# Two long attentions: row maxima taken in parts of 512 keys from two shared banks, keys loaded earlier, and a chunk's end moved to later steps of VectorE

## The reference, cut to what matters

```python
def gqa_attend(q, k, v):
    s = jnp.einsum('bqhgd,bkhd->bhgqk', q, k).astype(jnp.float32) * (GQA_HEAD_DIM ** -0.5)
    p = jax.nn.softmax(s, axis=-1).astype(v.dtype)
    return jnp.einsum('bhgqk,bkhd->bqhgd', p, v)

def mla_attend(q_nope, q_rope, k_nope, k_rope, v):
    s = (jnp.einsum('bqhd,bkhd->bhqk', q_nope, k_nope)
         + jnp.einsum('bqhr,bkr->bhqk', q_rope, k_rope)).astype(jnp.float32) * ((MLA_NOPE + MLA_ROPE) ** -0.5)
    p = jax.nn.softmax(s, axis=-1).astype(v.dtype)
    return jnp.einsum('bhqk,bkhd->bqhd', p, v)
...
    y = (o * jax.nn.silu(g)) @ p["w_out"]
```

## Time and profile before

| | us |
|---|---|
| median of 3 runs | 3574.1 (3573.39 to 3581.07) |
| the profiled execution's own time | 3577.36 |
| its span | 3575.6 |
| PE busy in the span | 3383.9 (95%) |
| DVE busy | 2187.7 (61%) |
| ACT busy | 1791.4 (50%) |
| POOL busy | 1534.0 (43%) |
| granted TensorE clock, mean | 0.989 |

### The profile page before, as it was taken

One profiled execution on the slowest core, in us unless ns is written; L12 is line 12 of the kernel. 1 busy time (PEld: TensorE's weight loads), 2 busy tenths in 40 slices (PEclk: granted clock), 3 DMA queues, 4 the chain that ended last, 5 costly groups with the idle time before them and its releaser, 6 DMA issues.

```text
span 3575.6 us, 48300 instructions
## 1 busy us (share of the span) xinstructions
PE 3383.9 (95%) x15156; PEld 2679.8 (75%) x15156; DVE 2187.7 (61%) x2655; ACT 1791.4 (50%) x3060; POOL 1534.0 (43%) x977
## 2 busy tenths in 40 slices
PE   7999999999999999999899999989988999999999
PEld 5777877778888888687777777768765667777777
DVE  6674877477575756447246666566558875555551
ACT  3343868242010101434158888861466657777870
POOL 3303444434444443510156666656210026666652
PEclk9999999999999999999999999999999999999999
DMA  2134232311212121123443433413255344232311
GB/s 99 53 118 120 72 80 75 126 42 63 78 57 86 55 91 36 58 102 115 119 95 66 103 80 81 94 62 100 97 198 154 118 116 122 54 82 53 76 42 71
DMA packets 196087, 313.54 MB, mean 88 GB/s; under 512 B 100928, under 2 KB 111680, under 8 KB 195968
## 3 DMA queue, kind: packets, MB, share of 16 engines
q1 hardware_dynamic: 195968, 312.01, 30.4%
HBM read 234.02 MB, written 77.92 MB: 87 GB/s over the span
## 4 chain that ended last, share of the span: by engine, by line
PE 67%; DVE 12%; issue 6%; ACT 6%; DMA 3%; POOL 3%; SPq 3%; DVEq 0%; ACTq 0%; POOLq 0%
PE PBX L281 10%; PE PBX L283 10%; PE PBX L282 10%; PE PMX L281 5%; PE PMX L282 5%; PE PMX L283 5%; PE PMX L1966 3%; PE PD L2007 2%; PE PD L868 2%; PE PD L2008 2%; PE PD L2009 2%; DVE gqa_m L2098 1%; SPq L1907 1%; DMA gqa_q<-qh_d 1%; PE PBX L1991 1%
## 5 line engine op out<-in xcount | busy, mean ns | idle before, releaser
L216 POOL TENSOR_TENSOR w_hi<-w_stage,zero 128x1024 fp32r<-128x1024 f32 (+2 forms) x123 | 227.7, 1851 | 1261.0 <-PE PBX L283 784.9
L2076 POOL TENSOR_TENSOR gqa_pl<-gqa_pf,gqa_ph 128x512 fp32r<-128x512 f32 (+1 forms) x288 | 370.7, 1305 | 188.4 <-ACT gqa_ph L2049 187.8
L2076 POOL TENSOR_TENSOR mla_pl<-mla_pf,mla_ph 128x512 fp32r<-128x512 f32 x256 | 351.9, 1384 | 205.6 <-ACT mla_ph L2049 201.5
L2098 DVE TENSOR_REDUCE gqa_m<-PMX 128x1 f32<-128x1280 f32 (+1 forms) x158 | 200.9, 1271 | 175.7 <-PE PMX L1966 175.0
L218 POOL TENSOR_TENSOR w_lo<-w_stage,w_hi 128x1024 fp32r<-128x1024 f32 (+2 forms) x123 | 299.9, 2438 | 9.7
L1691 ACT ACTIVATE conv_in<-PBX 128x512 f32<-128x512 f32 x66 | 39.5, 599 | 480.7 <-PE PBX L283 476.7
L2098 DVE TENSOR_REDUCE mla_m<-PMX 128x1 f32<-128x1280 f32 x126 | 187.4, 1487 | 87.7 <-PE PMX L1966 87.2
L2044 ACT ACTIVATE mla_pf<-PBX 128x512 f32<-128x512 f32 x320 | 189.8, 593 | 97.7 <-PE PBX L1992 84.6
L2044 ACT ACTIVATE gqa_pf<-PBX 128x512 f32<-128x512 f32 (+1 forms) x352 | 201.9, 573 | 55.3 <-PE PBX L1995 51.2
L2049 ACT ACTIVATE gqa_ph<-gqa_pf 128x512 fp32r<-128x512 f32 (+1 forms) x352 | 215.6, 613 | 13.8
L281 PE MATMUL PBX<-ffn_hi,w_hi 128*128 128x512 f32 x528 | 206.8, 392 | 3.8 <-DVE ffn_lo L665 3.8
(11 more groups left out here) (415 smaller groups left out, 9977.3 us busy)
## 6 DMA issues: line engine op xcount, KB each, us to landing
mod_w<-in_w_mod SPq DMA_DIRECT2D x48, 512.0 KB, 3.5
w_stage<-in_w_up SPq DMA_DIRECT2D x44, 512.0 KB, 3.4
w_stage<-in_w_go SPq DMA_DIRECT2D x24, 512.0 KB, 3.8
gqa_k<-kh_d SPq DMA_DIRECT2D x32, 320.0 KB, 5.0
gqa_q<-qh_d SPq DMA_DIRECT2D x32, 320.0 KB, 7.6
w_stage<-in_w_down SPq DMA_DIRECT2D x24, 384.0 KB, 3.1
qh_d<-heads_qh SPq DMA_DIRECT2D x32, 256.0 KB, 2.0
ql_d<-heads_ql SPq DMA_DIRECT2D x32, 256.0 KB, 2.3
```

Of the source, the lines that this page charges most:

```text
L216: pool.tensor_tensor(w_hi[s][:, 0:st.cols], w_stage[s][:, 0:st.cols], z, ALU.add).then_inc(w_hi_done, 1)
L2076: eng.tensor_tensor(self.PL[k % 4][:, 0:n], self.PF[k % 4][:, 0:n], self.PH[k % 4][:, 0:n].bitcast(F32), ALU.subtract).then_inc(self.lo_dv ...
L2098: dve.tensor_reduce(self.M[g % 2][:, t:t + 1], MX[:, 0:w], AX.X, ALU.max, negate=True)\
```

## The change

- **Maxima in parts.** `max` tasks now name a part (0, 1, 2) of at most 512 keys, and each part is a unit of its own. PE writes a unit into one of the two banks `MX` (the first two of `PMX`), alternating by the unit's number, and waits for the reduction of the unit two before it. DVE reduces each part (L2127) into `M[:, t, part]`; after the last part of a chunk a small reduction over `M` gives the negated maxima `NEG` (L2133). Part 0 stands in one step, parts 1 and 2 in the next. One tile of chunk 1 is moved up behind the maxima of chunk 0.
- **Broadcast and row.** The broadcast also goes into a bank of `MX` as a unit, and DVE instead of ACT copies its row into Q (L2144).
- **Banks.** The banks set free serve as score banks (`S`: 3 in GQA, 4 in MLA) and as a third output bank in GQA. The rings of `PF`, `PH`, `PL` have 6 buffers in GQA and 5 in MLA, before 4. `LAG` is 4, before 3.
- **Short chunk.** The two steps of GQA's third chunk, 256 columns each, become one step whose operations on ACT and POOL are 512 wide; PE's products stay the same.
- **Ends.** DVE runs `final` at `END_LAG` steps after the chunk's last step: 9, 8 and 10 in GQA, 8 and 7 in MLA. `T` is gone: the product with `RD`, which has two halves now, goes straight into `MIX`, and the gate multiplies in place.
- **Loads.** K and the high part of Q are loaded when the scores of the head before end (`scores`), and maxima wait only for these (`loaded_max`); the low part of Q and V follow after `pv` and, for the odd head, after `fin` and the gate; the first scores wait for them (`loaded`).

```diff
-            LAG = 3
+            LAG = 4
...
-                self.S = [PB[0], PB[1]]
-                self.BC = PB[2]
-                self.FREE = self.BC
-                self.O = [PD[0], PD[1]]
+                self.S = [PB[0], PB[1], PB[2]] + [PMX[:, 2 * C:3 * C]] * self.mla
+                self.NS, self.NP = len(self.S), len(self.PF)
+                self.O = [PD[0], PD[1], PMX[:, 2 * C:3 * C]][:len(chunks)]
+                self.MX = [PMX[:, 0:C], PMX[:, C:2 * C]]
+                self.FREE = self.S[0]
+                self.END_LAG = (8, 7) if self.mla else (9, 8, 10)
...
+                def tiles(at, first, count, step):
+                    return [(step + 2 * t + min(p, 1), "max", at, first + t, p) for t in range(count) for p in range(3)]
 
...
-                    plan = [(2 * t, "max", (0, 1), t) for t in range(4)] + [(8, "bcast", (0, 1), 0)]
-                    plan += [(8 + 2 * t, "max", (0, 2), t) for t in range(2)] + [(12, "bcast", (0, 2), 0)]
-                    plan += [(12 + 2 * t, "max", (1, 0), t) for t in range(4)] + [(21, "bcast", (1, 0), 0)]
+                    plan = tiles((0, 1), 1, 3, 0) + [(7, "row", (0, 1), 0, 0)]
+                    plan += [(7 + t, "max", (0, 2), t, 0) for t in range(2)] + [(10, "row", (0, 2), 0, 0)]
+                    plan += tiles((1, 0), 0, 4, 10) + [(19, "row", (1, 0), 0, 0)]
+                    plan += tiles((1, 1), 0, 1, 19)
...
-                    sp.wait_ge(self.pv, i * self.SB + CR_PV2)
-                    self.load_kv(sp, 1, kv_row(i, 1))
+                    sp.wait_ge(self.scores, i * self.SB + CR_SC)
+                    self.load_k(sp, 1, kv_row(i, 1))
                     self.load_q(sp, 1, i * 2 + 1)
+                    sp.wait_ge(self.pv, i * self.SB + self.NP)
 
                     sp.wait_ge(self.fin, i * (2 * self.NC) + CR_FIN2)
                     sp.dma_start(self.G[:, :], gate_d[bass.ds(i, 1), :, 0:self.nq].rearrange("o p n -> (o p) n"))\
                       .then_inc(self.gate_loaded, 16)
+                    self.load_q_lo(sp, 1, i * 2 + 1)
+                    self.load_v(sp, 1, kv_row(i, 1))
...
-                    pe.wait_ge(self.red, i * (2 * self.NT) + (tile + free))
...
+                    if unit >= len(MX):
+
+                        pe.wait_ge(self.red, i * (2 * self.NU) + (unit - len(MX) + 1))
...
+                def row(i, q, c, unit):
+                    o, n = self.chunks[c]
+                    r = self.row
+                    dve.wait_ge(self.max, i * R + (unit + 1))
+                    dve.tensor_copy(self.Q[q][0 if self.mla else 1][r:r + 1, o:o + n], self.MX[unit % 2][r:r + 1, 0:n])\
                        .then_inc(self.red, 1)
...
+                lag = max(self.END_LAG)
+
+                def ends(i, k):
+                    for e, (q, c, _, _, last_) in enumerate(self.steps):
+                        if last_ and e + self.END_LAG[c] == k + lag:
+                            final(i, e)
+                self.run(dve, step, ends, lag=lag)
```

More of the change, by code:

```diff
@@ L2011, in pe @@
-                for t in range(4):
-                    maxima(0, 0, 0, t, t, t == 0, 0, (PMX, PBX)[t % 2], CR_R - min(t, 1))
-                keep_clock(pe, self.O[0], 9)
-                bcast(0, 0, 0)
+                        pe.wait_ge(self.norm, i * (2 * NC) + (q * NC + c - NC + CR_N + 1))
+                    o = self.O[c][:, 0:n]
+                    for j, t in enumerate(tiles):
+                        ph, pl = [X[k % self.NP][:, j * n:j * n + n] for X in (self.PH, self.PL)]
+                        pe.matmul(o, self.V[q][0][:, t, :], ph, start=first and j == 0, stop=False)
+                        pe.matmul(o, self.V[q][1][:, t, :], ph, start=False, stop=False)
+                        mm = pe.matmul(o, self.V[q][0][:, t, :], pl, start=False, stop=last_ and j == len(tiles) - 1)
@@ new lines, in values @@
+                    mm.then_inc(self.pv, 1)
+                for t in range(4):
+                    for p in range(3):
+                        maxima(0, 0, 0, t, p, 3 * t + p, t == 0 and p == 0, 0, self.MX + self.S)
+                        if 3 * t + p >= 4:
+                            keep_clock(pe, self.O[0], 1)
+                keep_clock(pe, self.O[0], 5)
+                bcast(0, 0, 0, 12)
+                for p in range(3):
+                    maxima(0, 0, 1, 0, p, 13 + p, False, 0)
@@ L2016, in step @@
                 def step(i, k, last):
-                    for kind, q, c, t, g, tile, over in self.tasks(k, last):
+                    for kind, q, c, t, part, group, unit, over in self.tasks(k, last):
                         if kind == "max":
-                            maxima(i, q, c, t, tile, c == 0 and t == 0, i + 1 if over else i)
+                            maxima(i, q, c, t, part, unit, c == 0 and t == 0 and part == 0, i + 1 if over else i)
                         else:
-                            bcast(i, c, g)
+                            bcast(i, c, group, unit)
```

277 lines of the change are left out of this document (141 added, 136 removed).

## The result

The changed kernel takes **3614.0 us** (median of 4 runs, 3609.83 to 3618.82) against 3573.8 us for the kernel before on the same chip: a ratio of **1.0109, 95% interval 1.0095 to 1.0123**. It is slower by 1.1%, where 3523 us and a gain had been forecast. Its profiled execution took 3609.83 us, span 3607.6 us, 32.0 us more than the span of before.

What follows compares the result with a forecast made beforehand. TensorE was taken to need 29.9 us of a 34.4 us GQA head and 33.1 of 34.6 in MLA, the rest being waits; -37 (GQA) - 18 (MLA) + 4 (start and end) = -51 us gave 3523 us, 8-in-10 range 3496 to 3555.

Steps and rivals of the forecast that it cites:

- Ends moved: DVE's chunk ends, GQA: run later, the reciprocal is ready and DVE's 63.9 us of waiting for it go.
- Maxima in parts: DVE's reduction of 1280 becomes 512, 512, 256: +0.32 us a tile, +2.5 us a head; PE waits for one part two back.
- Loads late: Rival: high parts land 2 us behind step 10, V eats the rest; 1 us a head lost, 3555 us; chance 0.09.
- Start and end of each stage: More reductions at the start, +1.5 us, and later values at the end, +0.5; +4 us for two stages.
- Where the new order makes PE wait: PE's waits behind DVE at fixed steps of a head: 2.2 us a GQA head, 0.4 us an MLA head.
- the sum: The forecast's addition for both attentions: -37 GQA, -18 MLA, +4 start and end, together -51 us.
- the walk: Step-by-step timing of DVE's order against PE's in a head, giving 32.1 us a GQA head, 33.5 an MLA head.
- DVE becomes the bound; slower: Rival: lower parts' waits for ACT and stretching beside POOL make a GQA head 35.4 us; +20, 3594 us; chance 0.08.
- 26.5 against 34.4: DVE's forecast work a GQA head in us against the present length of that head, leaving 7.9.
- MLA: -18 forecast: MLA attention: a head was to take 33.5 us, 1.1 less, which is -18 us for the stage.

Runs made afterwards that it cites:

- e5: Changed kernel with POOL computing only 64 of the 512 columns of each lower part, the rest left zero, so POOL is nearly idle: 3539.3 us, ratio 0.9899.
- e11: Changed kernel with an end's two multiplications exchanged, gate first in the output bank, so each has one operand in PSUM: 3580.9 us, ratio 1.0015.
- e3: Changed kernel with the ends 2 to 3 steps further behind (1 for the short chunk), away from the rows: 3581.3 us, ratio 1.0012.
- e4: Changed kernel with each end 4 steps after its chunk, about where it was before the change: 3783.8 us, ratio 1.0579.
- e8: Changed kernel with the row on ACT and another order of maxima, row, ends and DVE's lower parts in GQA: 3542.1 us, ratio 0.9908.
- e2: Changed kernel with the row of maxima copied by ACT again, into the same two shared banks: 3568.8 us, ratio 0.9974.
- e12: e8 with an end's two multiplications exchanged, so that each has one operand in PSUM: 3529.8 us, ratio 0.9881.

## Why the prediction was wrong

**What held.** *Ends moved*: the wait for the reciprocal went as forecast. *Maxima in parts*: 690 and 416 ns against 0.69 and 0.423; the row copy 689 ns against 0.69. The loads are hidden: PE has no wait for DMA, so *Loads late* is out. Of the places where PE waits, steps 7, 8, 11 and 20 were named; so was the danger that an end stands directly ahead of `row`. *Start and end of each stage* was too small: put at +4 us for both, what the stages take ahead of their first and behind their last score product grew from 11.6 to 16.5 us in GQA and from 13.6 to 16.4 in MLA, 7.7 in all.

**The step that failed** is *Where the new order makes PE wait*: it put 2.2 us a GQA head. Measured is (24.6 + 40.7 + 16.5) / 16 = 5.1 us, and 1.2 us of lower clock behind it: 4.1 us a head that the sum did not have, where the head came out 3.9 us longer than forecast (36.0 against 32.1). By step, each total divided by the 15 or 14 heads that have it, beside the same waits with POOL nearly idle (e5):

```
us a head, GQA   forecast   changed     e5
step 7               0.25       0.5    0.5
step 8               0.45       0.7    0.5
steps 10, 11          0.6       1.9    0.6
step 19                 0       0.5      0
step 20               0.9       1.1    0.5
step 0                  0       0.7      0
```

At step 19 the walk had the diagonal done 0.14 us before PE came (2.55 against 2.69), and it did not look at step 0 at all.

**Why it failed.** The walk was right for a DVE that POOL leaves alone: in e5 the same waits are 33.5 us, 2.1 us a head, and 0.3 more at step 20 in waits under 0.15 us. Only step 7 was too small by itself: its wait for the diagonal is the same in e5, so POOL is no part of it. But the walk's durations were means of the earlier trace rows, 0.83 and 0.80 us, and 0.68 for the gate's product. Those of before were mixtures. The lower part of the kernel before, min, median and max over its 64 in GQA:

```profile
L2076 DVE TENSOR_TENSOR gqa_pl<-gqa_pf,gqa_ph x64: 671/692/1779, 1834.5 to 2373.7; 128x512 fp32r<-128x512 f32 x64
```

A median of 692 with a maximum of 1779 is not a slow operation but a free one that is sometimes held. Of the 64, the 34 that POOL did not touch took 689 ns on the mean, the 14 that POOL's operation met only when they were already running 680, and the 16 that stood 1258. I read the mean, found it "not far from what one undisturbed costs", and took the trace to show little blocking. The Trainium skill (SBUF — State Buffer, § SBUF: two separate sides) has the rule: a DVE operation with two SBUF inputs and a GpSimd operation that reads SBUF exclude each other for a whole instruction, whichever starts first. The rows agree: a stretched operation ends a fixed 0.55 us (512 columns) behind POOL's, and e11 and e5 confirm both conditions, the two operands and the other engine. The prediction named the rule in a rival, and priced it there for the diagonals and lower parts alone; the product with the gate, the largest new item (17.0 us), was not in its list.

**Why the change made it worse**, from 12.9 to 55.3 us. Before, the end of a chunk waited for ACT's reciprocal. While ACT made that, it made no rounded copy, so POOL had nothing to do, and the gate's product, just behind, found it idle. The kernel before, in time:

```profile
2053.56 0.63 ACT L2061 ACTIVATE gqa_rd<-gqa_rd 64x512 f32<-64x512 f32 x1
...
2055.24 0.68 DVE L2122 TENSOR_TENSOR MIX<-gqa_t,gqa_gate 64x512 f32 x1 [0.25 <-DVE gqa_t L2117]
...
2056.71 2.97 POOL L2076 TENSOR_TENSOR gqa_pl<-gqa_pf,gqa_ph 128x512 fp32r<-128x512 f32 x2 [2.43 <-ACT gqa_ph L2049]
```

POOL is idle for the 2.43 us ahead of 2056.71, waiting for ACT, and DVE's product lies inside. Over all 48 it never stood:

```profile
L2122 DVE TENSOR_TENSOR MIX<-gqa_t,gqa_gate x48: 416/684/692, 1848.6 to 2380.7; 64x512 f32 x28, 64x256 f32 x14, 64x512 f32<-64x512 f32 x4, 64x256 f32<-64x256 f32 x2
```

With the end moved to where ACT and POOL run evenly, it meets POOL in nearly every case; the changed kernel:

```profile
L2158 DVE TENSOR_TENSOR MIX<-MIX,gqa_gate x48: 422/952/1115, 1860.2 to 2412.4; 64x512 f32 x28, 64x256 f32 x14, 64x512 f32<-64x512 f32 x4, 64x256 f32<-64x256 f32 x2
```

And the place is a bad one (e3): ahead of `row`, on which with two shared banks PE's next but one product depends. e4 shows the other side: ends near the reciprocals never stand for POOL, but wait 82.5 us for ACT.

**The rival that came nearest, and not by its own account.** *DVE becomes the bound; slower* had 3594 us, 20 below what was measured, and 0.08. Its price for stretching was 3 us a head; measured is (55.3 - 12.9) / 16 = 2.65 more than before. Its other half was wrong: the waits of lower parts for ACT did not grow (25.2 us; 28.2 before, by the idle column of the earlier trace rows), and DVE with 449 us busy in 594 is no bound. It needs none: DVE has slack in most steps, and PE still pays wherever its own fixed place behind DVE comes due. A comparison of sums a head, 26.5 against 34.4, could not see that.

**The lower clock was not in the sum.** At step 11 in the timeline PE waits 1.29 us, does two products of maxima, and then several at 0.42 to 0.43 us each. All such products lose 19.8 us in GQA, before 4.5; the stage's granted clock fell from 0.99 to 0.97. It goes down with the waits in most experiments (e5 11.2, e8 9.6) and up with them (e4 76.7), so I count it as a consequence of the waits; e3, with 62.5 us of waits and 23.2 of lower clock, is the exception.

**MLA: -18 forecast, -2 measured.** With the row on ACT it is -14 (552.3 against 566.2), with POOL out of the way -17; then a head takes 33.4 us, by the score products as above, where 33.5 was forecast. The row on DVE costs it 12 us. Nearly all of PE's wait is at step 19: 13.1 us in all behind the row and the part after it, gone in e2, e3 and e5 alike. So here too the end ahead of the row and POOL's holding act together. The gate's product is the smaller part of it: without its standing (e11, where the diagonals still stand 13.7 us) 7.3 us of that wait stay, and the stage gains 1.9 us only.

**What stays open.** Why the diagonal's standing at step 19 differs from head to head is only argued (its start against POOL's operations). For the diagonal itself nothing like e11's exchange was tried. How much of e12's 10 us beyond e8 is the wait and how much the shorter DVE order was not separated. e5 is 16 us above the forecast; some 11 us of lower clock in GQA and the larger start and end of the stages are what its trace has beyond the sum.

## What to carry to other kernels

In this kernel an operation of DVE with two operands in SBUF costs its own time only while POOL runs no operation that reads SBUF: read its minimum, median and maximum rather than its mean, and where PE waits behind it, give it an operand in PSUM or a place where POOL has nothing to do. Before moving work out of a wait, ask what else was idle because of that wait; the moved work may have lived from it. And a walk through the order must be made with the durations of the new surroundings, at the few steps where another engine waits, since slack summed over a head does not pay for them.

## What the runs showed of the hardware that was not expected

- A held operation of DVE does not take its whole time again after POOL's end: with 512 columns it ends 0.54 to 0.56 us behind (undisturbed 0.69), with 256 some 0.28 (undisturbed 0.42). About 0.14 us of it is done while it stands.
- The exclusion works both ways: 38 of POOL's 272 lower parts in the changed kernel's GQA took 1.70 us or more (up to 1.85), where an undisturbed one takes 1.29; at the start of each of the 38 a DVE operation with two operands in SBUF was running.
- Operations that write back into the PSUM bank they read (e11) cost no more than those that write to SBUF: 688 against 682 ns.
- PE's waits of 1.29 to 1.32 us at step 11 were followed by products at the lower clock level (0.42 us apart instead of 0.234) in 6 of the 14 heads, seven or eight products each, 8.5 us in all; in the other 8 heads the same wait was followed by none.
